# Sums of squares of k, q, fox q and fox k as two rounded TensorE passes in place of one full-precision product

## The reference

```python
def l2_normalize(x):
    return x * lax.rsqrt(jnp.sum(jnp.square(x), axis=-1, keepdims=True) + NORM_EPS)
...
    q = l2_normalize(q.reshape(B, Lp, GDN_HEADS, GDN_DK))
    k = l2_normalize(k.reshape(B, Lp, GDN_HEADS, GDN_DK))
...
    q = heads(rms_norm(q.reshape(B, L, FOX_HEADS, FOX_DH), q_norm_g))
    k = heads(rms_norm(k.reshape(B, L, FOX_HEADS, FOX_DH), k_norm_g))
```

## Time and profile before

| | |
|---|---|
| time, median of 3 runs | 2870.75 us (2870.59 to 2870.86) |
| profiled execution, its own time | 2874.62 us |
| its span, first to last instruction | 2872.8 us |
| mean granted TensorE clock | 0.991 |
| busy: TensorE, VectorE, ScalarE, GpSimd | 98%, 71%, 50%, 10% of the span |
| full-precision sums in the mixing stage | 80, each recorded as two matmul passes (160 records) |

### The profile page before, as it was taken

How to read it: one execution, slowest core, us unless ns; L and a number is a source line. 1 busy time by engine, 2 the same in 40 slices (tenths; PEclk the granted TensorE clock), 3 DMA queues, 4 the chain that set the end, 5 groups by cost and what they waited for, 6 DMA issues and landing times.

```text
span 2872.8 us, 52171 instructions
## 1 busy us (share of the span) xinstructions
PE 2802.5 (98%) x18363; PEld 2534.7 (88%) x18363; DVE 2039.7 (71%) x3720; ACT 1429.0 (50%) x2482; POOL 294.2 (10%) x261
## 2 busy tenths in 40 slices
PE   7999999999999899999999999999999999999998
PEld 7999999999999788888888888888888998888876
DVE  5777778777777566657775665656777766778875
ACT  4655655565566444344453443534545554445542
POOL 0000000000000000003620000000460002400024
PEclk8999999999999999999999999999999999999999
DMA  5444343444444355556555555555555444544444
GB/s 194 143 138 147 128 149 132 153 135 142 141 144 136 128 186 189 183 190 213 182 185 192 181 190 180 186 193 184 192 177 174 159 168 145 190 162 147 146 140 169
DMA packets 130240, 474.91 MB, mean 165 GB/s; under 512 B 15136, under 2 KB 15136, under 8 KB 129952
## 3 DMA queue, kind: packets, MB, share of 16 engines
q1 hardware_dynamic: 126144, 459.46, 47.7%
q0 software_dynamic: 3936, 13.34, 1.5%
HBM read 470.49 MB, written 2.25 MB: 165 GB/s over the span
## 4 chain that ended last, share of the span: by engine, by line
PE 87%; DVE 7%; issue 3%; POOL 2%; ACT 1%; DMA 1%; DVEq 0%; POOLq 0%; ACTq 0%
PE bank L305 34%; PE bank L306 17%; PE bank L307 9%; PE bank L308 8%; PE bank L309 8%; DVE mix_solve_m L1897 2%; DVE w_lo L281 1%; PE bank L773 1%; PE bank L818 1%; POOL late_sum L454 1%; POOL late_sq L450 1%; DVE mix_part L1878 1%; DVE mix_inv L1875 1%; PE bank L1027 1%; ACT w_hi L275 1%
## 5 line engine op out<-in xcount | busy, mean ns | idle before, releaser
L281 DVE TENSOR_TENSOR w_lo<-raw,w_hi 128x1024 fp32r<-128x1024 f32 x866 | 1063.6, 1253 | 169.0 <-ACT w_hi L275 166.3
L275 ACT ACTIVATE w_hi<-raw 128x1024 fp32r<-128x1024 f32 x866 | 899.9, 1052 | 467.2 <-PE bank L306 450.8
L305 PE MATMUL bank<-u,w_hi 128*128 128x512 f32 x2288 | 819.0, 400 | 0.1
L305 PE MATMUL bank<-ya,w_hi 128*128 128x512 f32 x1792 | 639.4, 401 | 12.3 <-DVE w_lo L281 4.7
L307 PE MATMUL bank<-u,w_hi 128*128 128x272 f32 (+2 forms) x2064 | 638.6, 309 | 8.7 <-DVE w_lo L281 6.8
L306 PE MATMUL bank<-u,w_lo 128*128 128x256 f32 x2288 | 644.2, 282 | 0.0
L309 PE MATMUL bank<-u,w_lo 128*128 128x272 f32 (+2 forms) x2064 | 591.0, 286 | 0.0
L308 PE MATMUL bank<-u,w_hi 128*128 128x272 f32 (+2 forms) x2064 | 590.9, 286 | 0.0
L305 PEld LDWEIGHTS bank<-u,w_hi 128*128 128x128 f32 x2288 | 430.8, 188 | 98.6 <-issue 2.8
L306 PE MATMUL bank<-ya,w_lo 128*128 128x256 f32 x1792 | 505.6, 282 | 0.0
L306 PEld LDWEIGHTS bank<-u,w_lo 128*128 128x128 f32 x2288 | 432.6, 189 | 0.5
(11 more groups left out here) (385 smaller groups left out, 3217.3 us busy)
## 6 DMA issues: line engine op xcount, KB each, us to landing
raw<-in_stream SPq DMA_DIRECT2D x868, 512.0 KB, 3.4
mix_row<-rows POOLq DMA_DIRECT2D x16, 408.0 KB, 3.8
xT<-in_xT SPq DMA_DIRECT2D x4, 544.0 KB, 5.6
mix_coef_m<-meta_rows POOLq DMA_DIRECT2D x16, 128.0 KB, 3.5
h<-in_xT POOLq DMA_DIRECT2D x1, 2048.0 KB, 9.5
out_dram<-h SPq DMA_DIRECT2D x4, 512.0 KB, 2.6
consts<-in_consts POOLq DMA_DIRECT2D x1, 1817.0 KB, 9.2
meta_rows<-mix_b_mat POOLq DMA_DIRECT2D x16, 1.0 KB, 2.5
```

Source lines behind the costliest of these rows:

```text
L275: act.activation(w_hi[:, slot], raw[:, slot], ACT.Copy).then_inc(hi_ready, 1)
L281: dve.tensor_tensor(w_lo[:, slot], raw[:, slot], w_hi[:, slot].bitcast(F32), ALU.subtract).then_inc(lo_ready, 1)
L305: pe.matmul(o, a, x, start=first, stop=False)
```

## The change

Four of the five sums of a head (all but o) take two one-pass matmuls in place of the full-precision one. ScalarE's square now writes a rounded high part `sq_hi`; GpSimd squares the same tile in full into `sq_all`; VectorE subtracts, `sq_rest` = `sq_all` - `sq_hi`, written over `sq_all`; TensorE multiplies rounded ones (`ones_r`, a copy made once by ScalarE) with `sq_hi` and adds the product with `sq_rest`, for which it waits between the two.

VectorE gets four steps more in its plan ("k rest" at 70, "q rest" at 86, "fq rest" at 96, "fk rest" at 110), each ahead of the step that stood there but "fq rest", which is behind level 0. In TensorE's plan the fk sum goes from 110 to 111, and `prod` 2 (111) now stands ahead of it. GpSimd's squares of k, q and fox q stand ahead of a head's coefficient transfers, that of fox k behind them. Each waits for the sum before it. The factor 0.5 of k and q moves from the square into the logarithm (0.25). `decay` and `decay_t` now lie over `g_diff`, for which `g diff` has two more waits on the head before. A few semaphores of the later attention stages are merged; their waits are on the same events.

```diff
-        sq, rs_t = mt("sq", [P, TOK]), mt("rs", [P, TOK])
+        ones_r = mt("ones_r", [P, P], F32R)
+        sq, sq_all, rs_t = mt("sq", [P, TOK]), mt("sq_all", [P, TOK]), mt("rs", [P, TOK])
+        sq_hi, sq_rest = mt("sq_hi", [P, TOK], F32R, over="sq"), mt("sq_rest", [P, TOK], F32R, over="sq_all")
...
-        g_exp, decay, decay_b = mt("g_exp", [P, TOK]), mt("decay", [P, TOK]), mt("decay_b", [P, FOLD])
-        decay_t = mt("decay_t", [P, P])
+        g_exp, decay_b = mt("g_exp", [P, TOK]), mt("decay_b", [P, FOLD])
         g_diff, qk = mt("g_diff", [P, TOK + P]), mt("qk", [P, TOK])
+        decay, decay_t = g_diff[:, 0:TOK], g_diff[:, TOK:]
...
-            (105, "prod", 1), (106, "fq sum"), (109, "step", 1), (110, "fk sum"), (111, "prod", 2), (118, "logits"),
+            (105, "prod", 1), (106, "fq sum"), (109, "step", 1), (111, "prod", 2), (111, "fk sum"), (118, "logits"),
...
-            (63, "silu", "k"), (70, "unit k"), (72, "g diff"), (72, "fox bias"), (78, "silu", "z"), (85, "decay b"),
-            (86, "b mat"), (90, "unit q"), (92, "qk"), (94, "q dec"), (96, "level", 0), (98, "mask", 1),
-            (110, "unit fq"), (111, "level", 1), (111, "unit fk"), (113, "mask", 2), (114, "logits"),
+            (63, "silu", "k"), (70, "k rest"), (70, "unit k"), (72, "g diff"), (72, "fox bias"), (78, "silu", "z"), (85, "decay b"),
+            (86, "q rest"), (86, "b mat"), (90, "unit q"), (92, "qk"), (94, "q dec"), (96, "level", 0), (96, "fq rest"), (98, "mask", 1),
+            (110, "unit fq"), (110, "fk rest"), (111, "level", 1), (111, "unit fk"), (113, "mask", 2), (114, "logits"),
...
+            def square_whole(name, n, src, width):
+
+                at_ = norm_of_head(name, n)
+                if name == "gdn k" and n > 1:
+                    gp.wait_ge(sem("length sum"), at_ - 2)
+                elif at_ > 1:
+                    gp.wait_ge(sem("length sum"), at_ - 1)
+                gp.tensor_tensor(sq_all[:, :width], src, src, ALU.mult).then_inc(sem("length whole"), 1)
+
             head_rows(1)
             for n in range(1, HEADS + 1):
+                gp.wait_ge(sem("silu"), n * 4 - 1)
+                square_whole("gdn k", n, kT[:], TOK)
+                square_whole("gdn q", n, qT[:, META:], SEQ)
+                b, turn = head_tile("fq", n)
+                gp.wait_ge(tile_free[b], turn + 2)
+                square_whole("fox q", n, fq[:], SEQ)
                 meta_coefficients(n)
+                b, turn = head_tile("fk", n)
+                gp.wait_ge(tile_free[b], turn + 2)
+                square_whole("fox k", n, fk[:], TOK)
...
-                pe.matmul(bank[2][:, :width], const("ones"), sq[:, :width], start=True,
+                if name == "gdn o":
+                    pe.matmul(bank[2][:, :width], const("ones"), sq[:, :width], start=True,
+                              stop=True).then_inc(sem("length sum"), 1)
+                    return
+                if n == 1:
+                    pe.wait_ge(sem("norm hi"), KT + 1)
+                pe.matmul(bank[2][:, :width], ones_r[:], sq_hi[:, :width], start=True, stop=False)
+                pe.wait_ge(sem("length rest"), rest_of_head(name, n))
+                pe.matmul(bank[2][:, :width], ones_r[:], sq_rest[:, :width], start=False,
                           stop=True).then_inc(sem("length sum"), 1)
...
+            act.activation(ones_r[:], const("ones"), ACT.Copy).then_inc(sem("norm hi"), 1)
...
-            def square(name, n, src, width, pre):
-
-                act.activation(sq[:, :width], src, ACT.Square, scale=pre).then_inc(sem("length sq"), 1)
+            def square(name, n, src, width):
+
+                o = sq if name == "gdn o" else sq_hi
+                act.activation(o[:, :width], src, ACT.Square).then_inc(sem("length sq"), 1)
...
+                    dve.wait_ge(sem("decay beta"), n - 1)
+                    dve.wait_ge(sem("qk decayed"), n - 1)
...
+            def square_rest(name, n, width):
+
+                dve.wait_ge(sem("length whole"), rest_of_head(name, n))
+                dve.wait_ge(sem("length sq"), norm_of_head(name, n))
+                dve.tensor_tensor(sq_rest[:, :width], sq_all[:, :width], sq_hi[:, :width].bitcast(F32),
+                                  ALU.subtract).then_inc(sem("length rest"), 1)
```

More of the change, by code:

```diff
@@ L231, in __init__, with __call__ @@
             def __init__(self, tag, spans):
-                self.tag, self.spans = tag, [list(s) for s in spans]
-            def __call__(self, name, shape, dt=F32):
+                self.tag, self.spans, self.where = tag, [list(s) for s in spans], {}
+            def __call__(self, name, shape, dt=F32, over=None):
+                if over is not None:
+                    return nc.alloc_sbuf_tensor_at(f"{self.tag}_{name}", list(shape), dt, offset=self.where[over])
                 size = -(-int(np.prod(shape[1:])) * 4 // 64) * 64
@@ L237, in __call__ @@
                     if s[0] + size <= s[1]:
+                        self.where[name] = s[0]
                         s[0] += size
@@ L519, in program, with rest_of_head @@
         MB = 2 * MIX_TILES
+        def rest_of_head(name, n):
+            return n * 4 - 3 + ("gdn k", "gdn q", "fox q", "fox k").index(name)
         def norm_of_head(name, n):
@@ L1014, in _ @@
                         if g and not k:
-                            pe.wait_ge(sem("c ln"), 1)
+                            pe.wait_ge(sem("c root"), 1)
                         pe.matmul(bank[2][:, :SEQ], const("ones"), norm_sq[:, k, :SEQ], start=k == 0,
@@ L1281, in act_k_square @@
                     act.wait_ge(sem("length rs"), norm_of_head("gdn o", n - 1))
-                square("gdn k", n, kT[:], TOK, 0.5)
+                square("gdn k", n, kT[:], TOK)
             def act_q_square(n):
@@ L1286, in act_q_square @@
                 act.wait_ge(sem("length rs"), norm_of_head("gdn k", n))
-                square("gdn q", n, qT[:, META:], SEQ, 0.5)
+                square("gdn q", n, qT[:, META:], SEQ)
             def act_fq_square(n):
@@ L1292, in act_fq_square @@
                 act.wait_ge(sem("length rs"), norm_of_head("gdn q", n))
-                square("fox q", n, fq[:], SEQ, 1.0)
+                square("fox q", n, fq[:], SEQ)
             def act_fk_square(n):
@@ L1298, in act_fk_square @@
                 act.wait_ge(sem("length rs"), norm_of_head("fox q", n))
-                square("fox k", n, fk[:], TOK, 1.0)
+                square("fox k", n, fk[:], TOK)
             def act_o_square(n):
@@ L1303, in act_o_square @@
                 act.wait_ge(sem("length rs"), norm_of_head("fox k", n))
-                square("gdn o", n, bank[6][:, 0:SEQ], SEQ, 1.0)
+                square("gdn o", n, bank[6][:, 0:SEQ], SEQ)
             def act_cols(n):
@@ L1333, in act_decay @@
                                    bias=neg_g[:, c:c + 1]).then_inc(sem("decay"), 1)
-                act.activation(decay_t[:], g_diff[:, TOK:], ACT.Exp, bias=col[:, 2, 1:2]).then_inc(sem("decay"), 1)
+                act.activation(decay_t, g_diff[:, TOK:], ACT.Exp, bias=col[:, 2, 1:2]).then_inc(sem("decay"), 1)
             def act_turned(n):
@@ L1399, in _ @@
             steps_act = {"columns": act_columns, "tanh": act_tanh, "k square": act_k_square, "cols": act_cols, "decay": act_decay,
-                         "k root": lambda n: root("gdn k", n, TOK, 1.0, ("gdn y", 2 * n - 2)),
+                         "k root": lambda n: root("gdn k", n, TOK, 0.25, ("gdn y", 2 * n - 2)),
                          "q square": act_q_square,
-                         "q root": lambda n: root("gdn q", n, SEQ, 1.0, ("unit k", n)),
+                         "q root": lambda n: root("gdn q", n, SEQ, 0.25, ("unit k", n)),
                          "turned": act_turned, "fq square": act_fq_square,
@@ L1534, in c_root @@
                 act.activation(norm_ln[:, :SEQ], bank[2][:, :SEQ], ACT.Ln, scale=1.0 / MLA_RANK,
-                               bias=const("eps")).then_inc(sem("c ln"), 1)
-                act.wait_ge(sem("c ln"), g + 1)
+                               bias=const("eps")).then_inc(sem("c root"), 1)
+                act.wait_ge(sem("c root"), 2 * g + 1)
                 if g:
                     act.wait_ge(sem("c v"), RT)
-                act.activation(norm_rs[:, :SEQ], norm_ln[:, :SEQ], ACT.Exp, scale=-0.5).then_inc(sem("c rs"), 1)
+                act.activation(norm_rs[:, :SEQ], norm_ln[:, :SEQ], ACT.Exp, scale=-0.5).then_inc(sem("c root"), 1)
             def c_high(g):
@@ L1555, in _ @@
                     act.wait_ge(sem("total ln"), 3)
-                    act.activation(late_sq[:, 1], late_ln[:], ACT.Exp, scale=-0.5).then_inc(sem("rs of gained"), 1)
+                    act.activation(late_sq[:, 1], late_ln[:], ACT.Exp, scale=-0.5).then_inc(sem("rs"), 1)
                 else:
@@ L1816, in dve_b_mat @@
                 dve.scalar_tensor_tensor(out=prod[:, META:], in0=bank[5][:, FOLD:TOK], scalar=col[:, 2, 0:1],
```

(14 more changed lines are left out.)

## The result

The changed kernel takes 2903.30 us (median of 5 runs, 2900.58 to 2903.88) against 2870.77 (5 runs) for the kernel before: ratio 1.011, 95% interval 1.0095 to 1.0125. That is 32.5 us slower; forecast were 27.5, with a range of 2876 to 2914.

What follows compares the result with a forecast made beforehand. TensorE, busy 98% of the span, was taken as the bound. Terms of +5.3 (k sum), +7.8 (q sum) and +14.4 (fq sum to prod 3) made +27.5 us on 2870.75, so 2898 us, range 2876 to 2914.

Steps and rivals of the forecast that it cites:

- The cheaper sum: TensorE's sums: two one-pass matmuls give back 0.21 or 0.195 us each, 12.9 us over 64 sums at most.
- k sum: VectorE's k rest stands behind y, so the second matmul waits: +0.37 us a head, 15 heads, +5.3 with the first.
- q sum: q rest and GpSimd's square of fq delay unit q on VectorE, so qk waits: +0.49 a head, +7.8 in all.
- not the full length: Shared port beside GpSimd's square: VectorE loses the rows' 0.4 us, not up to 0.62; q term 7.8, not 11.3.
- fq sum to prod 3: Late level 1, prod 2 ahead of the fk sum, then late logits and level 2: +0.90 a head, +14.4 us.
- Hidden subtractions: Rival: every subtraction is done before its second matmul and no chain gets longer; 2858 us, chance 0.05.
- swallowed delay: Rival: TensorE's earlier waits before prod 3 and prod 4 absorb 0.96 a head; +12.1, 2883 us, chance 0.13.
- Only k waits: Rival: k sum costs +5.3 and the three other sums give 9.6 back; 2866.5 us, chance 0.07.
- GpSimd is not last: Rival denied here: GpSimd's square of fk comes late behind the coefficient transfers; 2914 us with one us beyond cover, chance 0.10.

Runs made afterwards that it cites:

- two sums of 256 undisturbed: Against the changed kernel: only q and fox q rounded, unit q ahead of a w_lo step, fk sum ahead of prod 2; 2865.12 us, ratio to before 0.9979.
- the changed order: Changed kernel with only VectorE's order changed, k rest ahead of y: 2897.31 us, ratio to the kernel before 1.0086.

## Why the prediction was right

**The cheaper sum** (0.21 and 0.195 us saved) is right: two sums of 256 undisturbed gave 0.43 a head, where the sum gives 0.39. In the first head, where the k sum has no y before it, the 0.21 was forecast and 0.10 came.

**k sum, forecast +0.37 a head, measured +0.49.** The place, the cause (y) and the start of the second matmul (0.70 behind the first forecast, 0.72 measured) were right, shown by the undone k sum and by the changed order. Mis-sized was what follows a wait: the matmul that ends it takes 0.39 and the next starts 0.23 behind it, where I had put 0.13 (353.55 to 353.68). The idle time forecast was near 0.6 and the bracket shows 0.41; from start to start it is 0.72 in place of 0.12, so 0.60.

**q sum, forecast +0.49, measured +0.43 to qk and 0.1 for its restart.** Cover of 0.13, no wait at the sum itself and the wait at qk were right. The chain lost 0.30 to the port where I had put 0.4, and the restart that I had left out cost 0.1; that the two nearly cancel is luck. That moving unit q removes all of it shows that the chain on VectorE was the cause.

On the shared port the Trainium skill (SBUF — State Buffer, section "SBUF: two separate sides") states an exclusive lock for the whole instruction of the one that starts first. The trace agrees to within 0.14 us, if what was left of the square is counted and not its whole length. The step of the b mat chain starts 0.25 after the square of fq and has 0.43 of it still to run, and loses 0.30; w_lo starts 0.11 after that of fk, has 0.53 to run, and loses 0.38. The prediction saw "not the full length" in its rows, but they say the same: the square ends at 1354.55 + 1.53 = 1356.08 and the second w_lo, 1.22 alone, at 1354.38 + 2.77 = 1357.15, 1.07 later.

**fq sum to prod 3, forecast +0.90, measured +1.0** (in the eleven regular heads; 1.3 in the head shown, with the late exponential). Prod 2's wait was put at 0.9 and is 0.86, that of prod 3 at 0.4 to 0.8 and is 0.66. w_lo lost 0.38 to the square of fox k, not 0.28. The steps, their order and their dependence were right. The run with the fk sum ahead of prod 2 corrects one reading: I wrote that the swap makes TensorE wait, and it does, but unswapped TensorE waits 0.58 at the fk sum, so only part of the 0.9 is the swap's: undoing it gave back 0.58 a head.

**The sum.** 0.49 + 0.53 + 1.0 = 2.0 a head, 32 us, less 0.9 for the first head; forecast 1.76 and 27.5. The three terms were each small by 0.04 to 0.12, all on the same side, mostly the restarts. The two profiled executions differ by 29.1 only: the changed one stood 2.4 us ahead at the first k sum (67.24 against 69.60), before anything of the change but the copy of the ones had run. From 38 to 45 us TensorE's granted clock was 0.51 in the kernel before (about the lower of its two levels, 1.2 GHz) and 1.00 in the changed one.

**The rivals.** Hidden subtractions and a swallowed delay are refuted: undoing a part gave back its term to within 0.02 us (the k sum 0.47 of 0.49; unit q early 0.71, which is the 0.53 and the saving of 0.195 that is then kept), and no wait downstream grew. "Only k waits" is refuted by the waits at qk and prod 2. GpSimd is not last: behind the coefficient transfers its square of fox k still waits 0.84 us for TensorE in the head shown, the least of the 16, where the prediction had worked out a cover of 0.8 to 1.3.

## What to carry to other kernels

Here TensorE, at 98%, gains from a cheaper instruction only where the helper work of the cheaper form is ready at its place; what decides is the cover at each place in the timeline (0.13 us before qk, none behind y, some 0.5 before prod 2), not the helper's 29% of idle time over the span. A part with cover can be kept and the others left: two of four sums in the new form are faster than none, or than all four in any order tried. And a step added to a chain has its price downstream: the q sum itself never waited, the matmul six blocks behind it did.

## What the runs showed of the hardware

A matmul that TensorE starts after a wait costs the next one 0.1 us: it is 0.39 us long in place of 0.28, and the next starts 0.23 behind in place of 0.12. The same is to be seen at qk (0.71 for four parts after a wait, 0.60 without). GpSimd's square of k, which starts beside a w_lo step of VectorE, took 1.48 us; that of q, which met none, 0.61. In all 16 heads of the changed kernel the w_lo step that starts 0.10 to 0.13 behind GpSimd's square of fox k ends 1.08 us after that square's recorded end, and alone it takes 1.22: when the square ended, 0.14 of it was done. The b mat step that starts behind the square of fox q (0.29 alone) ends 0.15 after that square in 15 of the 16 heads, the same 0.14.
